# Two feed-forwards whose input projections take seven block products instead of eight

## What is computed

```python
# second block, x is (1024 tokens, 1024) after a layer norm (ln1)
gate = sigmoid(x @ w_ple_gate)            # 1024 -> 1024, times p @ w_ple_proj
h = x @ w_ffn_in                          # 1024 -> 2 * 2816
ff = (silu(one half of h) * other half of h) @ w_ffn_out   # 2816 -> 1024
# third block
x = layer_norm(x + mix, ln1_g, ln1_b)
ff = square(relu(x @ w1 + b1)) @ w2 + b2  # 1024 -> 4096 -> 1024
x = layer_norm(x + ff, ln2_g, ln2_b)
```

## Time and profile before

| | us |
|---|---|
| median of 3 runs | 4087.46 (4087.4 to 4087.57) |
| the profiled execution's span | 4072.5 |
| TensorE busy in it | 3847.0 (94%) |
| DVE, ACT, POOL busy | 1730.0, 1302.6, 469.9 |
| opening of the second block's feed-forward | 1462 to 1538 |
| the rest of that feed-forward | 1538 to 2330 |
| opening of the third block's feed-forward | 3302 to 3356 |
| the rest of that feed-forward | 3356 to 4035 |

### The profile page before, as it was taken

How to read it: one execution, slowest core, us unless ns; L and a number is a source line. 1 busy time by engine, 2 the same in 40 slices (tenths; PEclk the granted TensorE clock), 3 DMA queues, 4 the chain that set the end, 5 groups by cost and what they waited for, 6 DMA issues and landing times. The chain is left out here.

```text
span 4072.5 us, 52923 instructions
## 1 busy us (share of the span) xinstructions
PE 3847.0 (94%) x21004; PEld 3035.7 (75%) x21004; DVE 1730.0 (42%) x2847; ACT 1302.6 (32%) x2309; POOL 469.9 (12%) x334
## 2 busy tenths in 40 slices
PE   9998999989997889999999999999788889999998
PEld 5787887867666768888888757767577768888886
DVE  3343423134566644222222355666566553333234
ACT  4354222123565342111101164555333231111112
POOL 1000000020004030000000231112424130000001
PEclk9999999999999999999999999999889899999999
DMA  2001111121112111111111112111201111111111
GB/s 91 29 31 55 32 49 44 47 87 32 41 31 89 41 43 47 46 52 47 46 52 45 37 44 69 51 52 52 95 33 33 37 32 47 52 47 47 52 47 58
DMA packets 87425, 199.46 MB, mean 49 GB/s; under 512 B 18873, under 2 KB 20345, under 8 KB 87241
## 3 DMA queue, kind: packets, MB, share of 16 engines
q1 hardware_dynamic: 87240, 196.96, 15.6%
HBM read 183.75 MB, written 15.14 MB: 49 GB/s over the span
## 5 line engine op out<-in xcount | busy, mean ns | idle before, releaser
L460 ACT ACTIVATE b_ffn_wh<-b_ffn_raw 128x1024 fp32r<-128x1024 f32 (+1 forms) x136 | 141.9, 1044 | 612.1 <-PE b_ffn_space L431 612.1
L430 PE MATMUL b_ffn_space<-b2f_x_lo,b_ffn_wh 128*128 128x512 f32 x800 | 314.9, 394 | 0.0
L429 PE MATMUL b_ffn_space<-b2f_x_hi,b_ffn_wh 128*128 128x512 f32 x800 | 312.8, 391 | 0.0
L431 PE MATMUL b_ffn_space<-b2f_x_hi,b_ffn_wl 128*128 128x512 f32 x800 | 312.8, 391 | 0.0
L521 DVE TENSOR_TENSOR b_ffn_wl<-b_ffn_raw,b_ffn_wh 128x1024 fp32r<-128x1024 f32 (+2 forms) x140 | 179.1, 1280 | 214.0 <-ACT b_ffn_wh L460 183.0
L429 PE MATMUL b_ffn_space<-b3f_hidden_hi,b_ffn_wh 128*128 128x512 f32 x512 | 199.2, 389 | 0.0
L430 PE MATMUL b_ffn_space<-b3f_hidden_lo,b_ffn_wh 128*128 128x512 f32 x512 | 199.2, 389 | 0.0
L431 PE MATMUL b_ffn_space<-b3f_hidden_hi,b_ffn_wl 128*128 128x512 f32 x512 | 199.2, 389 | 0.0
L430 PE MATMUL b_ffn_space<-b3f_x_lo,b_ffn_wh 128*128 128x512 f32 x480 | 189.3, 394 | 0.0
L429 PE MATMUL b_ffn_space<-b3f_x_hi,b_ffn_wh 128*128 128x512 f32 x480 | 187.3, 390 | 0.5 <-DVE b_ffn_wl L521 0.5
L431 PE MATMUL b_ffn_space<-b3f_x_hi,b_ffn_wl 128*128 128x512 f32 x480 | 186.9, 389 | 0.0
(11 more groups left out here) (679 smaller groups left out, 9079.5 us busy)
## 6 DMA issues: line engine op xcount, KB each, us to landing
b_ffn_raw<-w SPq DMA_DIRECT2D x62, 512.0 KB, 3.5
b_ffn_raw<-w_ffn SPq DMA_DIRECT2D x44, 512.0 KB, 3.5
all_x<-xT SPq DMA_DIRECT2D x16, 512.0 KB, 7.6
b_ffn_raw<-w_ffo SPq DMA_DIRECT2D x16, 512.0 KB, 3.6
g_heads<-na_done SPq DMA_DIRECT2D x16, 512.0 KB, 2.8
b3m_ahead<-w_gqkv SPq DMA_DIRECT2D x24, 256.0 KB, 3.3
b_ahead<-w_qk SPq DMA_DIRECT2D x16, 256.0 KB, 2.7
sgu_feed_raw<-w_au SPq DMA_DIRECT2D x16, 256.0 KB, 2.6
```

Source lines behind the costliest of these rows:

```text
L429: nc.tensor.matmul(acc[i][:, c], wh[i][:, wk], xh[:, c], start=(k == 0), stop=False)
L430: nc.tensor.matmul(acc[i][:, c], wh[i][:, wk], xl[:, c], start=False, stop=False)
L431: last = nc.tensor.matmul(acc[i][:, c], wl[i][:, wk], xh[:, c], start=False, stop=(k == st.KT - 1))
L460: nc.scalar.activation(wh[i][:, 0:st.KT * P], raw[i][:, 0:st.KT * P], ACT.Copy).then_inc(hi_done, 1)
```

## The change

The input projections are rewritten as block products. A pair of output blocks is a 2x2 block problem: weights A11, A12 (block one, first and second four input blocks), A21, A22 (block two), inputs B11, B21 (left half, first and second four input blocks), B12, B22 (right half). Eight products of 4 input blocks and 512 tokens give the four outputs C11 to C22; the rewriting makes them of seven, 12 matmuls each:

- weight sums S1 = A21 + A22, S2 = S1 - A11, S3 = A11 - A21, S4 = A12 - S2, made by POOL (`FastWeights.adding`), four per pair, and rounded and split like other weights;
- input sums T1 = B12 - B11, T2 = B22 - T1, T3 = B22 - B12, T4 = (B21 - B11) - T3, once per feed-forward: T1, T2, T3 on DVE (`FastLeadInputs.sums`), B21 - B11 (called left) and the last sums of T4, the fourth input, on POOL (`left_sums`);
- products A11 B11, A12 B21, S2 T2, S3 T3, A22 T4, S1 T1, S4 B22 in this order, except that the first two pairs run A11, A11, A12, A12 first;
- outputs put together on DVE out of eight PSUM banks of 128x512: C11 = A11 B11 + A12 B21 (A11 B11 is first copied out by ACT), u = A11 B11 + S2 T2, v = u + S3 T3, C21 = v + A22 T4, C22 = v + S1 T1, C12 = u + S1 T1 + S4 B22. That makes seven DVE instructions of 128x512 per pair.

All work of the feed-forwards is written out; no loops are left in them. Weights are loaded per pair (two tiles of 128x1024, two sets), and derived into seven slots of 128x512. x without its bias is copied to DRAM before the sums overwrite it (`copies`), and comes back for the residual. Hidden blocks are stored to DRAM and loaded back into the seven input buffers, 14 units of one hidden block, for the output projections (`FastHidden`), whose matmuls are as many as before. The embedding stays in the second block's opening; `Embedding.EACH`, the planned distance of its blocks, goes from 3.4 to 3.7. The plan starts product 0 at 22.0 and product 4 at 45.0 in the second block, at 20.0 and 36.0 in the third (in the plan's own time, which weave sorts by).

The core of the diff; lines of only "..." stand for what is left out:

```diff
-    KT, AT, EACH = 2, 7.5, 3.4
+    KT, AT, EACH = 2, 7.5, 3.7
...
+FAST_ORDER = ("A11", "A12", "S2", "S3", "A22", "S1", "S4")
+FAST_FIRST, FAST_REST = FAST_ORDER[:2], FAST_ORDER[2:]
+FAST_INPUT = {"A11": "B11", "S2": "T2", "A12": "B21", "S3": "T3", "S1": "T1", "A22": "T4", "S4": "B22"}
...
+FAST_PREPARED = ("B11", "B21", "T2", "T3", "T4", "T1", "B22")
...
+        self.order = [(s, o) for o in FAST_FIRST for s in (0, 1)] + [(s, o) for s in (0, 1) for o in FAST_REST]
+        self.order += [(s, o) for s in range(2, pairs) for o in FAST_ORDER]
+        self.ups = len(self.order)
+        self.first_block = [sum(chunks[:c]) for c in range(len(chunks))]
+        self.order += [(self.group(c, j), piece) for c in range(len(chunks)) for j in range(DT // 2) for piece in FAST_PIECES]
...
+        return {"A11": raw[:, 0, 0:HALF], "A12": raw[:, 0, HALF:S], "A22": raw[:, 1, HALF:S], "S3": raw[:, 1, 0:HALF],
+                "S1": self.sums_of[0][:], "S2": self.sums_of[1][:], "S4": self.sums_of[1][:]}[o]
...
+    def derived_at(self, n):
+        if n < self.slots:
+            return self.begin + self.step * n
+        return max(self.plan.at[n - self.slots + 1] + 0.3, self.begin + self.step * n)
...
+    def adding(self, pool):
+        for s in range(self.plan.pairs):
+            pos, raw = self.plan.pos, self.raw[s % 2]
+            a11, a12, a21, a22 = raw[:, 0, 0:HALF], raw[:, 0, HALF:S], raw[:, 1, 0:HALF], raw[:, 1, HALF:S]
+            s1, s2 = (t[:] for t in self.sums_of)
+            first = min(pos[s, o] for o in ("S1", "S2", "S3"))
+            at = self.derived_at(first) - 4.5
+            yield at
+            pool.wait_ge(self.landed[s % 2], 32 * (s // 2) + 32)
+            if s:
+                pool.wait_ge(self.low_done, pos[s - 1, "S1"] + 1)
+            self.nc.gpsimd.tensor_tensor(s1, a21, a22, ALU.add).then_inc(self.summed, 1)
+            yield at + 1.4
+            if s:
+                pool.wait_ge(self.low_done, pos[s - 1, "S4"] + 1)
+            pool.wait_ge(self.summed, 4 * s + 1)
+            self.nc.gpsimd.tensor_tensor(s2, s1, a11, ALU.subtract).then_inc(self.summed, 1)
+            yield at + 2.8
+            self.nc.gpsimd.tensor_tensor(a21, a11, a21, ALU.subtract).then_inc(self.summed, 1)
+            yield self.derived_at(pos[s, "S2"]) + 1.8
+            pool.wait_ge(self.low_done, pos[s, "S2"] + 1)
+            self.nc.gpsimd.tensor_tensor(s2, a12, s2, ALU.subtract).then_inc(self.summed, 1)
...
+        self.full = {"T1": x[:, first, left], "T4": x[:, second, left], "T3": x[:, first, right], "B22": x[:, second, right],
+                     "B11": self.own[:, 0], "B21": self.own[:, 1], "T2": self.own[:, 2]}
...
+    def sums(self, ve):
+        full, summed = self.inputs.full, self.inputs.summed
+        for k in range(FAST_ROWS):
+            yield self.norm.sized(1, FAST_ROWS - 1) + 0.1 + 0.01 * k
+            ve.wait_ge(self.norm.scaled, DT + k + 1)
+            ve.wait_ge(self.inputs.ready["B11"], k + 1)
+            ve.wait_ge(summed["left"], k + 1)
+            if k % 2 == 0:
+                ve.wait_ge(self.copied[k // 2], 16)
+            self.nc.vector.tensor_tensor(full["T1"][:, k], full["T3"][:, k], full["T1"][:, k], ALU.subtract).then_inc(summed["T1"], 1)
+        for k in range(FAST_ROWS):
+            yield self.norm.sized(1, DT - 1) + 0.1 + 0.7 * k
+            ve.wait_ge(self.norm.scaled, DT + FAST_ROWS + k + 1)
+            ve.wait_ge(summed["T1"], k + 1)
+            self.nc.vector.tensor_tensor(full["T2"][:, k], full["B22"][:, k], full["T1"][:, k], ALU.subtract).then_inc(summed["T2"], 1)
+        for k in range(FAST_ROWS):
+            yield self.norm.sized(1, DT - 1) + 5.6 + 0.7 * k
+            ve.wait_ge(summed["T2"], k + 1)
+            if k % 2 == 0:
+                ve.wait_ge(self.copied[4 + k // 2], 16)
+            self.nc.vector.tensor_tensor(full["T3"][:, k], full["B22"][:, k], full["T3"][:, k], ALU.subtract).then_inc(summed["T3"], 1)
+    def left_sums(self, pool):
+        full = self.inputs.full
+        for k in range(FAST_ROWS):
+            yield self.norm.sized(0, FAST_ROWS + k) + 3.5
+            pool.wait_ge(self.norm.scaled, FAST_ROWS + k + 1)
+            pool.wait_ge(self.inputs.ready["B21"], k + 1)
+            if k % 2 == 0:
+                pool.wait_ge(self.copied[2 + k // 2], 16)
+            self.nc.gpsimd.tensor_tensor(full["T4"][:, k], full["T4"][:, k], full["T1"][:, k], ALU.subtract).then_inc(self.inputs.summed["left"], 1)
+        for k in range(FAST_ROWS):
+            yield self.norm.sized(1, DT - 1) + 7.8 + 0.7 * k
+            pool.wait_ge(self.inputs.summed["T3"], k + 1)
+            pool.wait_ge(self.inputs.summed["left"], k + 1)
+            self.nc.gpsimd.tensor_tensor(full["T4"][:, k], full["T4"][:, k], full["T3"][:, k], ALU.subtract).then_inc(self.inputs.summed["T4"], 1)
...
+        self.units = [(o, 2 * i) for o in FAST_PREPARED for i in range(2)]
...
+    def loads(self, sp):
+        for g in range(len(self.plan.blocks())):
+            yield self.plan.at[self.freed(g)] + 0.2
+            sp.wait_ge(self.used, self.freed(g))
+            self.stored(sp, g)
+            source = self.hidden[g * P:(g + 1) * P, :].rearrange("p (h s) -> p h s", h=2)
+            sp.dma_start(self.view(self.inputs.full, g), source).then_inc(self.landed[g % len(self.units)], 16)
...
+    BANKS = (0, 1, 6, 7, 4, 5, 2, 3)
...
+        self.read_by = {"A11": self.kept, "A12": self.c11_done, "S2": self.u_made, "S3": self.v_made, "A22": self.c21_done,
+                        "S1": self.w_made, "S4": self.c12_done}
...
+    def first(self, pe, lead_waits):
+        for n, (s, o) in enumerate(self.plan.order[:self.plan.ups]):
+            operand = FAST_INPUT[o]
+            w, acc, high, low = n % self.weights.slots, self.bank(s, o), self.inputs.high[operand], self.inputs.low[operand]
+            for k in range(FAST_ROWS):
+                yield self.plan.at[n] + self.plan.ROW * k
+                if k == 0:
+                    if n < 8:
+                        lead_waits(pe, n)
+                    else:
+                        before, by = self.plan.order[n - 8]
+                        pe.wait_ge(self.read_by[by], before + 1)
+                    pe.wait_ge(self.weights.low_done, n + 1)
+                if s == 0:
+                    pe.wait_ge(self.inputs.ready[operand], k + 1)
+                wk = slice(k * P, (k + 1) * P)
+                self.nc.tensor.matmul(acc, self.weights.wh[w][:, wk], high[:, k], start=(k == 0), stop=False)
+                self.nc.tensor.matmul(acc, self.weights.wh[w][:, wk], low[:, k], start=False, stop=False)
+                last = self.nc.tensor.matmul(acc, self.weights.wl[w][:, wk], high[:, k], start=False, stop=(k == FAST_ROWS - 1))
+            last.then_inc(self.weights.used, 1)
...
+    plan = FastPlan(PAIRS, KTS, {0: 22.0, 4: 45.0})
...
+def third_feed_forward(nc, name, d, consts, cols, x, y, block_sum):
...
+    plan = FastPlan(PAIRS, KTS, {0: 20.0, 4: 36.0})
...
+        def lead_waits(pe, n):
+            if n < 2:
+                pe.wait_ge(norm.centred, DT * n + DT)
+            elif n < 4:
+                pe.wait_ge(norm.rooted[n - 2], 1)
+            elif n < 6:
+                pe.wait_ge(norm.scaled, DT * (n - 4) + DT)
...
+                def combining():
+                    for s in range(PAIRS):
+                        tile = u[s % 2]
+                        yield plan.end(s, "S2") + 0.1
+                        products.ready(ve, s, "S2")
+                        ve.wait_ge(products.c11_done, s + 1)
+                        nc.vector.tensor_tensor(tile[:], tile[:], products.bank(s, "S2"), ALU.add).then_inc(products.u_made, 1)
+                        yield plan.end(s, "S3") + 0.1
+                        products.ready(ve, s, "S3")
+                        ve.wait_ge(products.u_made, s + 1)
+                        if s:
+                            ve.wait_ge(v_out, 16 * s)
+                        nc.vector.tensor_tensor(v[:], tile[:], products.bank(s, "S3"), ALU.add).then_inc(products.v_made, 1)
+                        yield plan.end(s, "A22") + 0.1
+                        products.ready(ve, s, "A22")
+                        ve.wait_ge(products.v_made, s + 1)
+                        if s:
+                            ve.wait_ge(t2_out, 16 * s)
+                        nc.vector.tensor_tensor(t2, v[:], products.bank(s, "A22"), ALU.add).then_inc(products.c21_done, 1)
+                        yield plan.end(s, "S1") + 0.1
+                        products.ready(ve, s, "S1")
+                        ve.wait_ge(products.c21_done, s + 1)
+                        nc.vector.tensor_tensor(v[:], v[:], products.bank(s, "S1"), ALU.add).then_inc(products.c22_done, 1)
+                        nc.vector.tensor_tensor(tile[:], tile[:], products.bank(s, "S1"), ALU.add).then_inc(products.w_made, 1)
...
-            project_chain(nc, "b2_ffn", stages, block_sum=(block_sum, base), lead_of=lead_of)
```

(4 more changed lines are left out.)

583 lines of the change are left out of this document (542 added, 41 removed).

## The result

The changed kernel takes 3999.23 us in the median of 4 runs (3993.44 to 4002.81) against 4087.43 (4082.95 to 4087.57): a ratio of 0.9784, with a 95% interval of 0.9771 to 0.9798, or 88 us less. The forecast was 4022.5 in a range of 3988 to 4062.

The account below looks back on a forecast made before the run. TensorE, busy 94% of the span, was taken as the bound. Matmuls -115.3, pace +12, third opening +26.5, second opening +12 gave -65; 4072.5 - 65 + 15 = 4022.5 us, own range 3997 to 4047, judged range 3988 to 4062.

Parts of the forecast that it names:

- Matmuls taken out: Input projections of second and third block's feed-forwards: 504 fewer matmuls at 0.2287 us each, -115.3 us.
- Pace: All 6120 remaining matmuls, now written out: 0.231 us apart against 0.229 in the loops, +12 us.
- The lower bound's row: Pace's lower bound: looped matmul of low hidden tile 389 ns against 394 for low input tile, at best -10 us.
- The third block's opening: DVE's 76 instructions take 48.3 us undisturbed, GpSimd sums add 11.2, clock 2: +26.5 us.
- The second block's opening: Same DVE work plus embedding matmuls; ninth product at 1551.7, +12 us with 1 for the clock, waits under 10.
- The steady stretch and the changeovers: Between openings DVE and POOL need 15.8 of PE's 19.2 us per pair: no cost; uncovered changeovers up to 8.4 each.
- The 15 us around the span: Runs' median 4087.46 against profiled span 4072.5: 15.0 us taken to lie around the span and stay.
- rival (a): Both openings hidden because DVE and POOL hardly meet: 13.4 + 0 instead of 38.5, 3997 us; chance 0.10.
- (b): Slower than before: DVE and POOL saturate the steady stretch, 21.7 us a pair against 19.2, 4127.5 us; chance 0.07.
- (c): Changeovers late because SP's queue holds a load behind another wait: 59 us at most, some 35 likely, 4058; chance 0.14.
- (e): Seven products don't shorten the chain because something else, such as a weight chain, sets it: near 4087 us; chance 0.05.
- (d): Remaining matmuls run at the written-out sgu feed's pace, 0.234: +22 us, 4044, inside the forecast's range; no separate chance.

Follow-up runs that it names:

- the kernel before with x placed: The kernel before the change with x allocated at byte 21248 of each partition instead of 16512, nothing else; 4073.04 us, ratio 0.9958.
- the filler of the sgu feed: Changed kernel with x at byte 21248, small tables sent first, and padding moving mixer feed weights to their input's offset within 2048 bytes; 3982.64 us, ratio 0.9742.
- gqa's with its filler exact: The kernel with the filler of the sgu feed, but gqa feed weights at offset 768 exactly instead of 800; 3983.83 us, ratio 0.9755.

## Why the prediction was right, and where it was off

**Matmuls taken out.** Right: 3528 with the new inputs (1176 triples) and 2592 with the reloaded blocks (864), -115.3 us.

**Pace.** The step that failed. It put the 0.231 of a written-out stretch against the loops' 0.229 down to written-out code and came to +12 us, "the row of the same tiles". It measured -3.4, with steps of 0.2279 where 0.229 to 0.233 had been given as the sign. The low part in x was that row's input too: behind every third matmul 234 ns, and that is a matter of where a tile starts: in the kernel before with x placed, the last 66 steps of that very opening are 226 or 227. The lower bound's row, 389 ns of a hidden tile against 394 of the tile in x, pointed at the cause: it was read as a bound and not asked why two tiles of one size differ. This term is 15.4 of the 23 us by which the forecast lies above the median; the openings are 2.7 of them, the stretches outside take off 2.3, and 7.6 are the difference between profiles and medians. (The bound from the earlier trace rows has a slip: six steps in 1.40 us are 0.233 and not 0.234 each, +28 and not +34. The trace's mean over that feed is 0.234 all the same.)

**The third block's opening.** Right in mechanism and size: 48.3 us undisturbed, 48.1 measured when GpSimd had nothing to do; 59.5 with blocking, 59.7 measured; +26.5 for the opening, +26.1 measured. DVE's 76 instructions are the ones counted, kind by kind; GpSimd's sums were 17 and not 16. The price of a sum came from the difference of a low part's median and its least time, 0.7 us, and is 0.68. Two small terms met by luck: the 2 us added for PE's clock don't show, since PE waits for DVE right up to the ninth product, whatever its clock; but the first scaling, put down as unchanged, comes 1.2 us later than before. And PE's wait ahead of T3's product is 5.3 us and not 8 to 12.

The Trainium skill's SBUF page (SBUF — State Buffer, section Who interferes with whom) lets the loser of the shared ports wait out the other's whole instruction. The runs agree in kind: instructions with two SBUF inputs pay and the scalings with one in PSUM do not. In size a sum of 1.3 us cost 0.68 and not 1.3. That it falls in part on scalings and combinations, which don't pay, would explain it; how much of each sum does was not measured.

**The second block's opening.** +12 forecast, +9.7 measured in an execution in which the clock stood at 1.00 behind the tables; with the same instructions it was some 4 us more in another. DVE sets it here too: 56.9 us from the first scaling to B22's last low part were forecast, with 16 sums, and 55.2 measured, with 13; step 108 follows 0.9 us behind. PE waits 8.9 us in all from the first scaling on, within the 10 of the forecast; 4.4 of them are for low parts of the embedding's weights on GpSimd (L1140), which the prediction had only as a load on DVE.

**The steady stretch and the changeovers.** Right: no wait of PE in either rest, no idle at a chunk's end.

**The 15 us around the span.** A misreading: the changed kernel's profiled run of 3993.44 us has a span of 3991.9, so 1.5 lie around it. The profiled execution of before was then one of about 4074 us, of a kernel whose runs on record lie between 4077 and 4097. The sum was not hurt, since a difference was carried over; but it was worked out on that one execution, and the medians differ by 7.6 us more than the profiles.

**Rivals.** The time lies next to rival (a)'s 3997, for another reason: (a) wanted openings that cost 13 us together and they cost 35.8, while the pace gave back what it had been charged. Whoever judged by the time alone would call (a) confirmed. (b) fell: the steady stretch bears even all of GpSimd's sums on DVE. (c) and (e) did not occur. (d), a pace of 0.234, fell too: that row is slow because its weights lie 352 past a multiple of 2048 and both parts of its input 768; with equal offsets it takes 227.

## What to carry to other kernels

Taking matmuls out of a stretch in which TensorE is always busy is worth their full pace, and the price is paid where the new inputs are made: count that engine's instructions from the first input to the last, and add what the neighbour on its ports takes. Work given to GpSimd beside a full DVE saves nothing when both read SBUF; here every sum moved off DVE cost it 0.68 us for 0.60. When two tiles of one shape have different times in one loop, look at their addresses before explaining it by the code around them: how far apart moving data and weights start is what to compare.

## What was not expected of the hardware

- A matmul's step depends on where its moving data start relative to the weights: 226.7 ns where the starts agree, 234 ns for a low part at 128 against weights at 768 (within 2048 bytes), 231 to 238 in a feed with 352 against 768. Putting one tile right took 7 us off the changed kernel's rests and 11 off the feed-forwards of the kernel before (14 by its medians); the filler of the sgu feed took another 6.1.
- Equal offsets within 2048 bytes are more than it takes. Elsewhere in the same programs tiles lie at other places, and there what counts is the distance, a multiple of 256 bytes or not. At 1536 for weights and both input parts (second block's mixer output) the steps are 226 to 227, so it is not the place 768 itself. In the third block's mixer output weights, high parts and the low part `b3m_mixd_lo` lie at 384, the low part `b3m_mixn_lo` at 768, 384 bytes off: 227 behind the first, 234 behind the second, here in the kernel before:

```profile
3285.32 0.39 PE L430 MATMUL b_out_space<-b3m_mixd_lo,b_out_wh 128*128 128x512 f32 x1
3285.54 0.39 PE L431 MATMUL b_out_space<-b3m_mixd_hi,b_out_wl 128*128 128x512 f32 x1
...
3286.68 0.40 PE L430 MATMUL b_out_space<-b3m_mixn_lo,b_out_wh 128*128 128x512 f32 x1
3286.92 0.39 PE L431 MATMUL b_out_space<-b3m_mixn_hi,b_out_wl 128*128 128x512 f32 x1
```

  And x's move turned two stretches round. The third block's head has its weights and its high parts at 384: its steps behind the low part in x were 227 with x at 128 (256 off) and are 233.5 with x at 768 (384 off). The second block's head has its weights at 1536: 233.7 with x at 128 (640 off), 227.8 with x at 768 (768 off). Of the distances read here, those that came out slow (384, 416 and 640, and 32 in the gqa feed) are no multiples of 256, and those that came out at 227 or 228 (0, 256 and 768) are; but the gla feed, and gqa's with its filler exact, are slow in part at 0. No kernel was made to test the 256.
- With x in its new place looped and written-out matmuls have the same pace, 0.22667 us in both.
- The same instructions in the second opening ran at a granted clock of 1.00 in one execution and 0.82 in another, behind gaps of 4.45 and 5.30 us: 84 against 72 matmuls in 15 us.
